# First stage of the delta rule's inverse: additions in place of masked copies, weights of pairs on GpSimd, diagonals written ahead

## The reference, cut to what matters

```python
decay = jnp.exp(jnp.where(incl, gcum[..., :, None] - gcum[..., None, :], -jnp.inf))
kb = kc * bc[..., None]
lower = jnp.where(strict, jnp.einsum("nbhid,nbhjd->nbhij", kb, kc) * decay, 0.0)
t_inv = triangular_solve(eye + lower, eye, left_side=True, lower=True, unit_diagonal=True)
u = jnp.einsum("nbhij,nbhjd->nbhid", t_inv, vc * bc[..., None])
w = jnp.einsum("nbhij,nbhjd->nbhid", t_inv, kb * jnp.exp(gcum)[..., None])
```

## Time and profile before

| What | Value |
|---|---|
| median of 3 runs | 2638.75 us (2630.27 to 2652.36) |
| the profiled execution's own time | 2628.75 us |
| its span | 2626.9 us |
| busy: TensorE, its weight loads | 2428.2 us (92%), 2038.7 us (78%) |
| busy: VectorE, ScalarE, GpSimd | 1356.8 us (52%), 883.4 us (34%), 269.9 us (10%) |
| DMA | 192.83 MB, mean 73 GB/s |

### The profile page before, as it was taken

One profiled execution on the slowest core, in us unless ns is written; L12 is line 12 of the kernel. 1 busy time (PEld: TensorE's weight loads), 2 busy tenths in 40 slices (PEclk: granted clock), 3 DMA queues, 4 the chain that ended last, 5 costly groups with the idle time before them and its releaser, 6 DMA issues.

```text
span 2626.9 us, 34274 instructions
## 1 busy us (share of the span) xinstructions
PE 2428.2 (92%) x14914; PEld 2038.7 (78%) x14914; DVE 1356.8 (52%) x1768; ACT 883.4 (34%) x1253; POOL 269.9 (10%) x212
## 2 busy tenths in 40 slices
PE   6996999999989899999999798799998898899997
PEld 4875897888857678888888486688787756688885
DVE  3658763238744462333333665875228754634444
ACT  5364243210245332222223436433320264322223
POOL 2026010000030210000000303301000030100001
PEclk8998999999999999999999899899999999999998
DMA  8212311222230112222222221340221122133331
GB/s 288 57 49 97 115 32 49 65 65 83 78 104 17 48 32 65 65 65 65 65 65 65 80 71 35 96 145 10 72 65 33 39 96 64 64 96 97 96 96 49
DMA packets 159260, 192.83 MB, mean 73 GB/s; under 512 B 18134, under 2 KB 129080, under 8 KB 158599
## 3 DMA queue, kind: packets, MB, share of 16 engines
q1 hardware_dynamic: 158128, 190.18, 22.4%
q0 software_dynamic: 704, 0.37, 0.1%
q10 hardware_dynamic: 279, 0.09, 0.0%
HBM read 182.19 MB, written 8.44 MB: 73 GB/s over the span
## 4 chain that ended last, share of the span: by engine, by line
PE 82%; DVE 11%; ACT 3%; issue 2%; SPq 1%; DMA 1%; POOL 0%; DVEq 0%; ACTq 0%
PE ps L1202 32%; PE ps L699 20%; PE ps L1171 4%; PE ps L729 2%; PE ps L898 2%; PE ps L904 2%; PE ps L1043 2%; PE ps L1120 2%; DVE region L1954 1%; PE ps L1010 1%; PE ps L1188 1%; PE ps L769 1%; DVE mixed L1822 1%; DVE region L1985 1%; PE ps L686 1%
## 5 line engine op out<-in xcount | busy, mean ns | idle before, releaser
L1202 PE MATMUL ps<-region_r 128*128 128x512 f32 (+1 forms) x1536 | 376.3, 353 | 0.0
L1202 PEld LDWEIGHTS ps<-region_r 128*128 128x128 f32 x1536 | 270.6, 188 | 40.9
L1202 PE MATMUL ps<-region_r,weights_r 128*128 128x512 f32 (+1 forms) x768 | 229.6, 353 | 0.0
L1202 PE MATMUL ps<-modulated_r,region_r 128*128 128x256 f32 (+1 forms) x720 | 215.2, 353 | 0.0
L1202 PE MATMUL ps<-mixed_r,region_r 128*128 128x256 f32 (+1 forms) x720 | 215.2, 353 | 0.0
L1202 PE MATMUL ps<-mixed_r,weights_r 128*128 128x256 f32 (+1 forms) x720 | 215.2, 353 | 0.0
L1653 DVE TENSOR_TENSOR weights_r<-weights,region_r 128x2048 fp32r<-128x2048 f32 x64 | 146.5, 2288 | 118.4 <-ACT region_r L1299 118.4
L699 PE MATMUL ps<-residual_r,weights_r 128*128 128x256 f32 (+1 forms) x576 | 160.6, 347 | 0.0
L1202 PEld LDWEIGHTS ps<-region_r,weights_r 128*128 128x128 f32 x768 | 144.3, 188 | 20.5
L1593 ACT ACTIVATE region<-ps,cst 128x768 f32<-128x768 f32 (+1 forms) x64 | 51.0, 798 | 322.1 <-PE ps L1202 311.3
L2091 DVE TENSOR_TENSOR region_r<-region 128x768 fp32r<-128x768 f32 (+1 forms) x64 | 52.8, 825 | 205.9 <-ACT region L1593 205.9
(11 more groups left out here) (347 smaller groups left out, 4992.1 us busy)
## 6 DMA issues: line engine op xcount, KB each, us to landing
weights<-in_w_mlp SPq DMA_DIRECT2D x64, 1024.0 KB, 5.4
weights<-in_w_ada SPq DMA_DIRECT2D x40, 1024.0 KB, 5.2
weights<-in_w_in SPq DMA_DIRECT2D x34, 1024.0 KB, 5.2
region<-in_w_ada SPq DMA_DIRECT2D x8, 1024.0 KB, 16.4
weights<-in_w_out SPq DMA_DIRECT2D x8, 1024.0 KB, 6.9
x_kept<-residual SPq DMA_DIRECT2D x2, 3072.0 KB, 12.4
region<-decays_kept SPq DMA_DIRECT2D x4, 1536.0 KB, 10.6
residual<-x_kept SPq DMA_DIRECT2D x2, 3072.0 KB, 10.6
```

The lines of the kernel that those rows point to most:

```text
L1202: last = mm(dst[:, CTX + a:CTX + b], w[:, k, m], r[:, a:b], start=(k == 0 and r is r_low), stop=(k == KB - 1 and w is low))
```

## The change

- The two masked copies of a chunk become additions into the same alternate views. The diagonals must then stand there before, and the pair matrix must have nothing but the elements that belong to size 1.
- GpSimd multiplies `partner` (the identity with neighbouring rows exchanged) by the pair weights into a new area `first_off` (area 2 of `region`); VectorE multiplies NT by it, in place. W is no longer used in this stage after the exp.
- The diagonals of TT move from ScalarE (eight instructions per chunk) to VectorE (two per chunk, twelve in all), after the unit-length products and before the stage.
- The semaphore of the small gate values is raised after the pair weights, and GpSimd waits for it.
- TensorE no longer waits for the end of the stage before size 2: its products of chunks 0 to 2 come before the last turn, and the first two modulation points come after them, points 2 and 3 after the second group.
- SyncE's decay transfers write area 2, so they wait for the last `first_u` and no more for the last spans.

```diff
--- before.py
+++ after.py
@@ -169,6 +169,7 @@
         vtok, ktok = chunks(6), chunks(5)
         NT, att = chunks(6), (chunks(7), chunks(3))
         decay0, decay1 = chunks(3), chunks(2)
+        first_off = chunks(2)
 
         def heads(ap):
             return ap.rearrange("p (h d) -> p h d", h=H)
@@ -294,7 +295,8 @@
         la_a, la_v, la_ready, gs_a, gs_v, gs_ready = (sem(n) for n in ("ba_exps", "ba_sums", "la_ready", "g_split", "g_diff", "g_ready"))
         lhs_ready, spans_out, spans_exp, p1_out, p1_done = (sem(n) for n in ("lhs_ready", "spans_out", "spans_exp", "p1_out", "p1_done"))
         rows_out, rows_copied, rows_kept, decays_in = (sem(n) for n in ("decay_rows_out", "decay_rows_copied", "decay_rows_kept", "decays_in"))
-        diag_a, diag_p, first_w, first_t, first_u = (sem(n) for n in ("diagonals_act", "diagonals_pool", "first_w", "first_t", "first_u"))
+        diag_a, diag_p, nt_ready, first_w, first_t, first_u = (
+            sem(n) for n in ("diagonals_act", "diagonals_pool", "nt_ready", "first_w", "first_t", "first_u"))
         r1_out, w_ready, qt_out, qt_copied, q_out, u_ready = (
             sem(n) for n in ("r1_out", "w_ready", "qt_out", "qt_copied", "q_out", "inverse_ready"))
         c1_out, c1_v, c1_a, c2_out, c2_v, c2_a = (sem(n) for n in ("corner1_out", "corner1_v", "corner1_a", "corner2_out", "corner2_v", "corner2_a"))
@@ -485,7 +487,7 @@
                         sp.wait_ge(rows_copied, l + 1)
                         sp.dma_start(kept.rearrange("(r t) -> r t", t=128), decay_rows).then_inc(rows_kept, 16)
                         sp.wait_ge(rows_kept, 16 * (l + 1))
-                        sp.wait_ge(spans_out, NC * (l + 1))
+                        sp.wait_ge(first_u, NC * (l + 1))
                         for d, area in ((1, 2), (0, 3)):
                             sp.dma_start(R[:, area, :].rearrange("p (c n) -> p c n", c=NC),
                                          kept.rearrange("(c d n) -> d c n", c=NC, d=2)[d].partition_broadcast(128)).then_inc(decays_in, 16)
@@ -591,8 +593,10 @@
                 for ci in range(3):
                     weigh(ci)
                 pool.wait_ge(l2_done, 8 * (l + 1))
+                pool.wait_ge(gs_ready, l + 1)
                 pool.wait_ge(gemm_out, out_number(l, "qkv", 11))
                 for ci in range(NC):
+                    times_columns(first_off[:, ci], partner, pair_beta[:, ci, :].unsqueeze(2).to_broadcast([128, H, 128]))
                     times_columns(INV[1][:, ci], ident, columns(beta, ci, 1)).then_inc(diag_p, 1)
                     if ci + 3 < NC:
                         pool.wait_ge(spans_out, base + ci + 1)
@@ -843,13 +847,13 @@
 
                 def first_turned(ci):
 
-                    pe.wait_ge(first_w, base + ci + 1)
                     if ci == 1:
                         pe.wait_ge(rows_copied, l + 1)
                     if ci >= 2:
                         pe.wait_ge(first_u, base + ci - 1)
+                    pe.wait_ge(first_w, base + ci + 1)
                     for h in range(H):
-                        last = tr(ps[:, 6 + ci % 2, 128 * h:128 * h + 128], W[ci][:, h, :], ident)
+                        last = tr(ps[:, 6 + ci % 2, 128 * h:128 * h + 128], first_off[:, ci, h, :], ident)
                     last.then_inc(first_t, 1)
                 for ci in range(NC):
                     Z, KK, QK = 3 * (ci % 2), 3 * (ci % 2) + 1, 3 * (ci % 2) + 2
@@ -870,7 +874,6 @@
                     last.then_inc(p1_out, 1)
                     if ci:
                         first_turned(ci - 1)
-                first_turned(NC - 1)
 
                 def token_rows(i):
 
@@ -886,24 +889,28 @@
                     last.then_inc(tok_out, 1)
 
                 first = ADA_GDN_AT[l]
-                pe.wait_ge(first_u, base + NC)
-                for k in range(2):
-                    ada_point(first + k, first)
                 for g, size in enumerate(SIZES):
                     lb0 = NC * (NS * l + g)
                     for ci in range(NC):
                         if g:
                             pe.wait_ge(u_ready, lb0 - NC + ci + 1)
+                        else:
+                            if ci == 3:
+                                first_turned(NC - 1)
+                            pe.wait_ge(p1_done, base + (NC - 1 if ci < 3 else NC))
+                            pe.wait_ge(first_u, base + ci + 1)
                         for h in range(H):
                             last = mm(ps[:, ci, 128 * h:128 * h + 128], NT[:, ci, h, :], inverse_alternate(ci, size, h), start=True, stop=True)
                         last.then_inc(r1_out, 1)
-                    ada_point(first + 2 * g + 2, first)
+                    for k in range(2 if g == 0 else 1):
+                        ada_point(first + (k if g == 0 else 2 * g + 2), first)
                     for ci in range(NC):
                         pe.wait_ge(w_ready, lb0 + ci + 1)
                         for h in range(H):
                             last = mm(ps[:, ci, 128 * h:128 * h + 128], W[ci][:, h, :], TT_alternate(ci, size, h), start=True, stop=True)
                         last.then_inc(qt_out, 1)
-                    ada_point(first + 2 * g + 3, first)
+                    for k in range(2 if g == 0 else 1):
+                        ada_point(first + (k + 2 if g == 0 else 2 * g + 3), first)
                     for ci in range(NC):
                         pe.wait_ge(qt_copied, lb0 + ci + 1)
                         for h in range(H):
@@ -1434,9 +1441,8 @@
                 for ci in range(NC):
                     act.wait_ge(spans_out, base + ci + 1)
                     af(W[ci], ps[:, 3 * (ci % 2), :].rearrange("p (h d) -> p h d", h=H), ACT.Exp, bias=zero_col).then_inc(spans_exp, 1)
-                    for dst, d in ((TT[0], 0), (TT[1], 1), (INV[0], 0)):
-                        for h in range(H):
-                            last = af(dst[:, ci, h, :], ident, ACT.Identity, bias=zero_col, scale=beta[:, ci, d, h:h + 1])
+                    for h in range(H):
+                        last = af(INV[0][:, ci, h, :], ident, ACT.Identity, bias=zero_col, scale=beta[:, ci, 0, h:h + 1])
                     last.then_inc(diag_a, 1)
 
                 def token_rows(i):
@@ -1796,15 +1802,20 @@
                 link(v.tensor_copy(gd[:, 3, :], gcum_held[:, 96:144]))
                 v.tensor_tensor(gd[:, 6, :], gd[:, 3, :], gd[:, 2, :], ALU.subtract).then_inc(gs_v, 1)
                 dve.wait_ge(gs_a, l + 1)
-                v.tensor_scalar(gd[:, 7, :], gd[:, 4, :], -1.0, None, ALU.mult).then_inc(gs_ready, 1)
+                v.tensor_scalar(gd[:, 7, :], gd[:, 4, :], -1.0, None, ALU.mult)
                 link(v.tensor_tensor(both_beta, beta, raw[:, 3], ALU.mult))
                 link(v.tensor_scalar(pair_beta, both_beta[:, :, 0, :], parity[:, 0:1], None, ALU.mult))
-                link(v.scalar_tensor_tensor(pair_beta, both_beta[:, :, 1, :], parity[:, 1:2], pair_beta, ALU.mult, ALU.add))
+                v.scalar_tensor_tensor(pair_beta, both_beta[:, :, 1, :], parity[:, 1:2], pair_beta, ALU.mult, ALU.add).then_inc(gs_ready, 1)
                 for u in range(4):
                     unit_length(u)
                 convolve(10)
                 for u in range(4, 8):
                     unit_length(u)
+                dve.wait_ge(conv_done, 12 * l + 11)
+                for ci in range(NC):
+                    for d in range(2):
+                        last = v.tensor_tensor(TT[d][:, ci], over_heads(ident), beta[:, ci, d, :].unsqueeze(2).to_broadcast([128, H, 128]), ALU.mult)
+                link(last)
                 dve.wait_ge(gemm_out, out_number(l, "qkv", 11))
                 link(v.memset(zlast[:, 0:2], 0.0))
                 link(v.memset(zlast[:, CTX + 2:CTX + 4], 0.0))
@@ -1813,27 +1824,30 @@
                 outs, base = chunks_out(l), NC * l
 
                 dve.wait_ge(silu_done, 12 * l + 11)
-                alone = over_heads(masks[:, 14, :]).rearrange("p h (n e r) -> p h n e r", e=2, r=1)
 
                 def first_inverse(ci):
 
                     dve.wait_ge(first_t, base + ci + 1)
-                    dve.wait_ge(diag_p, base + ci + 1)
-                    v.copy_predicated(inverse_alternate(ci, 1), alone, by_blocks(ps[:, 6 + ci % 2, :], 1)).then_inc(first_u, 1)
+                    dve.wait_ge(diag_a, base + ci + 1)
+                    at = inverse_alternate(ci, 1)
+                    v.tensor_tensor(at, by_blocks(ps[:, 6 + ci % 2, :], 1), at, ALU.add).then_inc(first_u, 1)
                 for ci in range(NC):
                     KK, QK = 3 * (ci % 2) + 1, 3 * (ci % 2) + 2
                     dve.wait_ge(spans_exp, base + ci + 1)
                     dve.wait_ge(p1_out, base + ci + 1)
-                    link(v.scalar_tensor_tensor(NT[:, ci], heads(ps[:, KK, :]), -1.0, W[ci], ALU.mult, ALU.mult))
```

(16 more changed lines are left out.)

## The result

Before, 2634.68 us (median of four runs, 2630.27 to 2652.36); changed, 2606.98 us (2602.03 to 2617.58, four runs). The ratio is 0.9893, with a 95% interval of 0.986 to 0.9925: faster by 1.1%, clear of no change; the 1% line lies inside the interval. A later measurement (e11_after_again) gave 0.9897 (0.9869 to 0.9926). The profiled execution took 2604.08 us against 2628.75, 24.7 less. The forecast was 2623 in a range of 2606 to 2648, so the time lies inside it, at its fast edge, and the size of the saving was forecast at little more than half.

A forecast was written before the change was run, and what follows sets the result against it. TensorE held 82% of the chain, so gains counted only where it stood still, as in the VectorE-paced first stage. Layer 0 -7.4 and layer 1 -9.2 made -16.6, taken as -16 from 2638.75: 2623 us, range 2606 to 2648.

The forecast's parts named there:

- Its own signs of being wrong: First stage and after: prediction wrong if additions are off by 0.3 us or more, or TensorE's load wait is missing.
- the diagonals near 1.4 us and the first NT at 199 to 200: Layer 0, ahead of the stage: expected signs, six to seven diagonals near 1.4 us after 188.8, then first NT.
- the rivals at -25 and -28: First stage additions at 0.61: -25, -28 without clock loss (chance 0.27); load before size 2 transposes unhindered: -28 (0.09).
- The two take turns: Before the stage: seven diagonals alternate with GpSimd's products at 1.44 us, 10.1 in all; VectorE starts 5.8 us late per layer.
- Its order isn't the bound: GpSimd in the first stage: its last diagonal comes at about 215, ahead of its use at 223.
- the fourth rival: First stage: turns cost more, GpSimd at 5.3 us per chunk sets the first three chunks' pace; -10, 2629; chance 0.05.
- Additions at 1.13: VectorE, first stage: each addition replacing a masked copy takes 1.13 us, about 4.2 us per chunk with waits.
- the ends were 0.61 and 2.27: First stage: bounds for an addition's price, from 0.61 us (never following the copies) to 2.27 (L1822's copy price).
- The load behind the decays: After the stage: modulation load 3 queues behind decay transfers, TensorE stands some 6 us, size 4 begins at T + 21.
- The decay products one size on: GpSimd's decay products shift later, moving TensorE's wait from before size 4 to its end: +2.1 layer 0, +0.7 layer 1.
- The clock, +1 each: TensorE in the first stage: waiting after two chunks lowers its granted clock, +1.0 us in each layer.

The follow-up runs named there:

- e11_after_again: The changed kernel itself, unedited, measured again on the same chip as the two combined-edit runs: median 2609.28 us, ratio 0.9897 to the kernel before.
- e1_linked: Changed kernel with each of VectorE's twelve TT diagonals waiting for the one before it: 2622.3 us in one run.
- e6_tt_half: Changed kernel with ScalarE making the TT diagonals of chunks 3 to 5, VectorE only those of 0 to 2: 2601.41 us, ratio 0.9879.
- e2_inv1_on_scalar: Changed kernel with the INV[1] diagonals made by ScalarE instead of GpSimd: 2601.87 us, ratio 0.9865.
- e4_masked_copies: Changed kernel with the two additions per chunk turned back into masked copies: stage 42.3 and 42.6 us; no whole time given.
- e8_other_views: Changed kernel with the TT addition contiguous and the inverse addition stepping 64 elements inside one tensor (wrong result): 0.66 and 1.09 us; no whole time given.
- e10_half_split: Changed kernel with ScalarE making TT diagonals of chunks 3 to 5 and the area 3 decay transfer issued early: 2595.01 us, ratio 0.9840.
- e9: Changed kernel with INV[1] diagonals on ScalarE instead of GpSimd and the area 3 decay transfer issued early: 2597.24 us, ratio 0.9834.
- e7: Changed kernel with the decay transfer into area 3 issued before the stage ends, only area 2 waiting for the last first_u: 2603.88 us, ratio 0.9879.

## Why the prediction came out as it did

The mechanism held: the stage was the path, cheaper additions shortened it, and the load behind the decays took part of it back. The size was short by 11 us over both layers (-16.6 summed, -28.0 measured by the stretch), as much as one term, counted once in each layer: the collision of the diagonals with GpSimd was put on VectorE, and it was GpSimd that paid. T is the stage's end, as in the prediction. Its own signs of being wrong (additions off by 0.3 us, no wait for the load) didn't come, but the diagonals near 1.4 us and the first NT at 199 to 200 didn't come either. The measured saving lies nearer to the rivals at -25 and -28 than to my -16, though not by what they said: the additions take 0.96 from start to start and not 0.61, and the load did stand behind the decays.

- **"The two take turns", 7 x 1.44 us, "VectorE is ready at about 199.5: 5.8 us late": the step that failed.** The diagonals took 0.61 each, the first NT came at 193.64, no later than before, and GpSimd's first product waited them out. In layer 1 the lateness was 0.7 us by GpSimd's start (before: first NT 4.1 us after it, after: 4.8). The term stands twice in the sum with 5.8, and should have been -0.1 and 0.7. I had the price from six additions of the earlier trace rows, each of which waits for its own copy from ScalarE; the diagonals wait for nothing, and e1_linked shows that a wait between them is what lets GpSimd in, at just that price. One reading was loose, without effect: the product at 231.55 didn't run alone, copies L1822 ran beside it, but at 236.32 in the changed kernel, with VectorE idle, it takes the same 1.26.
- **"Its order isn't the bound": wrong as well, with the other sign, and in layer 0 only because of the first error.** By ending my GpSimd sum at "its last diagonal comes at about 215, ahead of its use" I looked at the end of the list and not at its pace. Four products per chunk with turns are 5.34 us against VectorE's 4.2, and GpSimd began them 4 us late because the diagonals held it off. Within the stage that took back 1.0 and 2.4 us: 29.6 and 29.9 where I had 28.6 and 27.4 from its own start. e6_tt_half, where it starts in time, has no such wait in layer 0 and keeps some in layer 1. The mechanism is the fourth rival's (0.05, "sets the pace of the first three chunks"), at 5.3 us, in chunks 1 to 3; it did not make the change as small as that rival said, because it came in place of the late start and not on top of it.
- **Additions at 1.13: right in kind, some 0.17 too dear.** Most last 1.08 to 1.18 us, but the sum counts from start to start, and there they take 0.92 to 1.00, where three plain ones take 0.61; the first TT addition, beside GpSimd, lasts 1.84. In e2_inv1_on_scalar, where GpSimd's pace doesn't bind in layer 0, the stage takes 25.9 us where my sum had 28.6; 2.0 of these 2.7 us are the twelve additions. A chunk there takes 4.33 us while GpSimd is at work, 0.6 of it the turn of the product L1843, and 3.71 once GpSimd is done, against my 4.2 without turns. e4_masked_copies and e8_other_views show that it was the element alone in its place that had to be priced; the ends were 0.61 and 2.27.
- **The load behind the decays: right.** Forecast T + 21 with some 6 us of standing; measured 21.0 in layer 0, with 4.58 us of idle (4.86 in layer 1), the point at 1.93 and slow transposes. In layer 1 it was 22.2, where before it had been 21.9: +0.4 instead of -1.0, because the transposes there took 4.53.
- **The decay products one size on, +2.1 and +0.7: not in this execution, but in another.** From size 4 to size 32 took 51.1 us in layer 0 both before and after, and 49.4 in layer 1 both times. The wait did move one size on, to 1.46 us ahead of 262.38; the products behind it ran at the full clock in 5.62 us. I had taken the 7.25 us of the earlier trace rows for a property of size 4 and left it there. It belongs to the wait: at 259.6 to 266.8 of the kernel before, the granted clock was 0.76. In e11_after_again, the same kernel as the changed one, wait and low clock have moved on together, and layer 0 takes 53.5 us, 2.4 more than before. TensorE in e11 and in e10_half_split, then the window of these products in e11:

```profile
263.72 7.25 PE L903 MATMUL ps<-mixed,region 128*128 128x128 f32 x48 [2.18 <-DVE mixed L1867]
```

```profile
255.74 7.25 PE L905 MATMUL ps<-mixed,region 128*128 128x128 f32 x48 [2.39 <-DVE mixed L1872]
```

```profile
263.70:271.00 7.30, 7.28 (x52) 7.16 (x56) 6.31 (x10) 0.00 (x0) 6.76 (x6) 0.77 0.18 68
```

So this term is worth 0 or 2 us by the run. The length of the wait doesn't decide it. The products took 7.25 us, at 0.76 to 0.77, after waits of 1.87 (e4), 2.03 (e9, layer 1), 2.14 (e7, layer 1), 2.18 (e11), 2.21 (before), 2.39 and 2.50 us (e10, both layers); they took 5.62 us at 1.00 after 2.33 (e9, layer 0) and 2.37 (e7, layer 0). What does decide stays open.
- **The clock, +1 each: not there in the stage.** VectorE wasn't late, so the pause of TensorE that it was to follow didn't come.

In numbers, from forecast to measured, both layers: late start -11.0, pace +3.4, load +1.4, decay products -2.8, clock -2.0, together -11.0. The pace is what is left after the cheaper additions, some 2 us per layer. So -16.6 becomes -27.6. Measured are -28.0 in the stretches and +0.6 in their starts (-0.1 and +0.7), -27.4.

## What to carry to other kernels

A list without gaps on one engine stood here for one long instruction to the engine that shares its port: it cost its owner nothing and the other 4 us, so put such a list where the other's work isn't on the path. Turns were there to be priced only where the colliding instructions waited for something in between. When an engine gets more work in a stage, compare the pace per step of every engine, turns included, and not only the time at which its list ends. A transfer that must wait takes the loads behind it in its queue along, and letting one load pass only moves the wait on; sending the part that has no reason to wait removes it.

## What the hardware showed that I had not expected

- **Who holds the port.** GpSimd's product beside twelve VectorE products without gaps: 5.18 us. With a wait between them: 1.30, then 1.48. Where only the last 0.5 us of a list of six lay beside it (e6_tt_half): 1.41. Alone: 1.04. With the list of twelve and with that of six GpSimd's product ended 0.9 us after the list's last product. The Trainium skill, page "SBUF — State Buffer", section "Who interferes with whom", says that the one which issues first has the shared pair of ports for the whole instruction. By that alone GpSimd would get its turn after the first diagonal; here it got none until the list was over, so the trace goes beyond the rule. The section also says that a VectorE instruction with at most one input in SBUF doesn't contend with GpSimd, and here the trace agrees: L1833, with its other input in PSUM, takes 1.10 at 201.53 beside GpSimd's work and 1.09 at 1646.75 without it.
- **A single element per place costs a masked copy more than an addition.** With GpSimd at rest the copy into TT takes 2.43 in the kernel before and 2.61 to 2.63 in e4_masked_copies, where whole runs take 0.72; the addition takes 1.08 to 1.15, contiguous 0.66. With GpSimd beside it the copy takes up to 3.19 and the addition up to 1.84.
